# Norms in token halves, an entry block for the rounded operand, and entry parameters behind the first weights

## The reference, cut to what matters

```python
for i in range(2):                                    # first_block
    f = swiglu_ffn(rmsnorm(x, ffn1_norm_pre[i]), ffn1_w_in[i], ffn1_w_out[i])   # ffn1
    x = x + 0.5 * rmsnorm(f, ffn1_norm_post[i])       # post1
    h = rmsnorm(x, mix_norm_pre[i])                   # mix
    ...                                               # p = h @ mix_w_in[i]; delta net, conformer convolution
    x = x + rmsnorm(y, mix_norm_post[i])              # post
    f = swiglu_ffn(rmsnorm(x, ffn2_norm_pre[i]), ffn2_w_in[i], ffn2_w_out[i])   # pre2, ffn2
    x = x + 0.5 * rmsnorm(f, ffn2_norm_post[i])       # post2
h = rms_norm(x, norm1_g)                              # second_block, one layer
...                                                   # proj = h @ w_in; mLSTM and LRU branches
x = x + merged @ w_out
x = x + peer(rms_norm(x, norm2_g), ...)               # 8 heads, 16 experts each, gathered by index
return rms_norm(x, final_norm_g)
```

## Time and profile before

| | us |
|---|---|
| median of 3 runs | 2656.24 |
| the profiled execution | 2657.05 |
| its span, first to last instruction | 2655.8 |
| TensorE matmul busy | 2269.2 (85%) |
| VectorE busy | 1759.4 (66%) |
| ScalarE busy | 970.9 (37%) |
| POOL busy | 807.2 (30%) |

### The profile page before, as it was taken

The page is one execution under the profiler, slowest core; times in us unless marked ns, Lnnn a source line. Parts: engine busy times, 40 slices in busy tenths (PEclk is TensorE's granted clock), DMA queues, the critical chain, the costliest instruction groups (busy, mean ns, idle before and its releaser), DMA issues.

```text
span 2655.8 us, 34386 instructions
## 1 busy us (share of the span) xinstructions
PE 2269.2 (85%) x13786; PEld 1932.1 (73%) x13786; DVE 1759.4 (66%) x3266; ACT 970.9 (37%) x1550; POOL 807.2 (30%) x671
## 2 busy tenths in 40 slices
PE   6999999999999999999999999999898544444445
PEld 6998998998998998998998998888766211111111
DVE  5555894665556556894665555243429998989986
ACT  4345554454335435553454432342213111111111
POOL 1005772000000005771000000000007777777774
PEclk9999999999999999999999999999999677777767
DMA  6567994025554567993024554443249999999997
GB/s 212 183 179 129 188 167 131 33 74 177 183 183 160 188 171 129 187 174 117 33 94 155 184 190 144 141 139 106 74 150 399 419 419 419 419 418 418 419 419 314
DMA packets 316369, 560.29 MB, mean 211 GB/s; under 512 B 16296, under 2 KB 233394, under 8 KB 316210
## 3 DMA queue, kind: packets, MB, share of 16 engines
q1 hardware_dynamic: 242482, 289.63, 39.7%
q0 software_dynamic: 73728, 268.47, 24.9%
HBM read 557.00 MB, written 1.05 MB: 210 GB/s over the span
## 4 chain that ended last, share of the span: by engine, by line
PE 65%; DVE 13%; POOL 8%; DMA 7%; issue 3%; ACT 3%; SPq 0%; DVEq 0%; ACTq 0%; POOLq 0%
PE banks_to L853 11%; PE bank L451 7%; PE bank L452 7%; PE bank L453 7%; PE bank L360 6%; POOL proj L2539 5%; PE banks_and L360 4%; DMA proj<-in_peer_v,gdn_conv 4%; DMA weights<-in_peer_v,gdn_conv 3%; POOL weights L2539 3%; DVE banks_to L1054 3%; PE banks_and L451 3%; PE banks_and L452 3%; PE banks_and L453 3%; PE banks_to L1246 2%
## 5 line engine op out<-in xcount | busy, mean ns | idle before, releaser
L407 POOL TENSOR_TENSOR weights_low<-weights,weights_high 128x1024 fp32r<-128x1024 f32 x128 | 306.1, 2423 | 683.3 <-ACT weights_high L370 682.8
L453 PE MATMUL bank<-operand_hi,weights_low 128*128 128x256 f32 x1792 | 508.5, 284 | 0.0
L451 PE MATMUL bank<-operand_hi,weights_high 128*128 128x256 f32 x1776 | 505.2, 284 | 3.6 <-DVE operand_lo L797 3.3
L452 PE MATMUL bank<-operand_lo,weights_high 128*128 128x256 f32 x1776 | 503.6, 284 | 0.0
L370 ACT CAST weights_high<-weights 128x1024 fp32r<-128x1024 f32 x392 | 386.6, 1046 | 7.0 <-DMA weights<-in_ffn_w_in 6.7
L443 DVE TENSOR_TENSOR weights_low<-weights,weights_high 128x1024 fp32r<-128x1024 f32 x264 | 308.2, 1221 | 91.3 <-ACT weights_high L370 91.3
L451 PEld LDWEIGHTS bank<-operand_hi,weights_high 128*128 128x128 f32 x1776 | 339.1, 191 | 7.0 <-issue 4.7
L453 PEld LDWEIGHTS bank<-operand_hi,weights_low 128*128 128x128 f32 x1792 | 342.9, 191 | 0.0
L452 PEld LDWEIGHTS bank<-operand_lo,weights_high 128*128 128x128 f32 x1776 | 337.5, 190 | 1.3
L453 PE MATMUL banks_and<-operand_hi,weights_low 128*128 128x256 f32 x768 | 217.6, 283 | 0.0
L451 PE MATMUL banks_and<-operand_hi,weights_high 128*128 128x256 f32 x752 | 213.7, 284 | 3.6 <-DVE operand_lo L797 3.3
(11 more groups left out here) (524 smaller groups left out, 4402.6 us busy)
## 6 DMA issues: line engine op xcount, KB each, us to landing
weights<-in_ffn_w_in SPq DMA_DIRECT2D x88, 1024.0 KB, 5.1
weights<-in_mix_w_in SPq DMA_DIRECT2D x64, 1024.0 KB, 12.5
weights<-in_ffn_w_out SPq DMA_DIRECT2D x44, 1024.0 KB, 5.0
weights<-in_w_in SPq DMA_DIRECT2D x24, 1024.0 KB, 5.3
weights<-in_cnv_w_o SPq DMA_DIRECT2D x8, 1024.0 KB, 6.5
weights<-in_gdn_w_o SPq DMA_DIRECT2D x8, 1024.0 KB, 5.2
weights<-in_mix_w_out SPq DMA_DIRECT2D x8, 1024.0 KB, 5.0
weights<-in_peer_w_q SPq DMA_DIRECT2D x8, 1024.0 KB, 5.7
```

Source lines behind the costliest of these rows:

```text
L407: S.rest.by(X.gpsimd.tensor_tensor(halves(m.low[b % SLOTS])[q], halves(m.raw[b % SLOTS])[q], halves(mix_high(m, l, i))[q].bitcast(F32), AL ...
L451: t.matmul(out, w_hi, x_hi, start=start, stop=False, skip_group_check=skip)
L452: t.matmul(out, w_hi, x_lo, start=False, stop=False, skip_group_check=skip)
L453: return t.matmul(out, w_lo, x_hi, start=False, stop=stop, skip_group_check=skip)
```

## The change

Six edits, which touch every boundary.

1. The post-norm interleaves the token halves: VectorE gains half 1 between the two adds of half 0.
2. The norm of the new residual is made for each token half apart (`vector_token_norm`, `scalar_token_norm`): a mean, a root, a reciprocal and a diagonal for each h. In the FFNs it moves ahead of the rounding and the rest of block 2, at the start ahead of those of block 1.
3. The scaled turn goes by pairs of tiles, (0, 1) of both h and then (2, 3) of both h, and all filler products stand before it (20; 12 at norm2). The plain turn keeps its order, with 10 filler products before and 5 between (8 and 8 before).
4. `operand_hi` signals each tile. Block 0 of an FFN or mixer (`tensor_entry_block`) first runs the 32 passes that read the rounded operand, k by k, both column halves, and then the 16 that read `operand_lo`. One clearing flag stands for the whole bank.
5. At the start SP asks for the parameters between weight blocks 0 and 1. TensorE turns the residual first, then 12 filler products, then the parameters, in other banks. VectorE's masks move behind the rest of block 1.
6. POOL computes the rest of a mixer's block 1 only when the post-norm's last add is done.

```diff
+def tensor_entry_block(X, m, S, b, high, low, n):
+    bank, x = b % BANKS, m.split_x
+    X.bank_free(bank)
+    out = lambda q: m.bank[bank][:, q * NT:(q + 1) * NT]
+    for q in range(2):
+        X.pe.wait_ge(*low.at(b, q))
+    for k in range(KT):
+        X.pe.wait_ge(*S.x_high.at(n, k))
+        for q in range(2):
+            hi, lo = halves(high)[q], halves(m.low[b % SLOTS])[q]
+            X.tensor.matmul(out(q), hi[:, k, :], x.hi[:, k, :], start=k == 0 and q == 0, stop=False, skip_group_check=True)
+            X.tensor.matmul(out(q), lo[:, k, :], x.hi[:, k, :], start=False, stop=False, skip_group_check=True)
+    for k in range(KT):
+        if k % 2 == 0:
+            X.pe.wait_ge(*S.x_low.at(n, k // 2))
+        for q in range(2):
+            ins = X.tensor.matmul(out(q), halves(high)[q][:, k, :], x.lo[:, k, :], start=False, stop=k == KT - 1, skip_group_check=True)
+    S.used.by(ins, b)
...
+    vector_gain_branch(X, m, S, n, ready, c, 0)
+    vector_add_branch(X, m, S, n, 0, 0)
+    vector_gain_branch(X, m, S, n, ready, c, 1)
+    vector_add_branch(X, m, S, n, 0, 1)
+    vector_add_branch(X, m, S, n, 1, 0)
+    vector_add_branch(X, m, S, n, 1, 1)
...
+def scalar_token_norm(X, m, S, n, ready, scratch):
+    scalar_token_squares(X, m, S, n, 0, ready, scratch)
+    scalar_token_squares(X, m, S, n, 1, ready, scratch)
+    scalar_token_root(X, m, S, n, 0)
+    scalar_token_root(X, m, S, n, 1)
+
+def vector_token_norm(X, m, S, n):
     for h in range(2):
+        vector_token_mean(X, m, S, n, h)
+    for h in range(2):
+        vector_diagonal(X, m, S, n, h)
...
     tensor_keep_going(X, m, before, first % BANKS)
-    tensor_turn(X, m, S, n, 0, first, ready, scaled)
-    tensor_keep_going(X, m, between, first % BANKS)
-    tensor_turn(X, m, S, n, 1, first, ready, scaled)
+    if scaled:
+        for pairs in ((0, 1), (2, 3)):
+            for h in range(2):
+                tensor_turn(X, m, S, n, first, ready, scaled, h, pairs)
+    else:
+        tensor_turn(X, m, S, n, first, ready, scaled, 0, range(4))
+        tensor_keep_going(X, m, before // 2, first % BANKS)
+        tensor_turn(X, m, S, n, first, ready, scaled, 1, range(4))
...
-    tensor_params(X, m, S, 0)
     for l in range(LAYERS):
-        tensor_to_split(X, m, S, ("pre1", l), ("ffn1", l), x_ready_at(S, l), False, 8, 8 if l else 0)
-        tensor_ffn(X, m, S, ("ffn1", l), split_at(S, ("pre1", l)))
+        tensor_to_split(X, m, S, ("pre1", l), ("ffn1", l), x_ready_at(S, l), False, 10 if l else 0)
+        if not l:
+            tensor_keep_going(X, m, 12, 1)
+            tensor_params(X, m, S, 0)
+        tensor_ffn(X, m, S, ("ffn1", l))
...
-        for i in range(AHEAD):
-            pool_mix_rest(X, m, S, l, i)
-        for i in range(AHEAD, MIX_BLOCKS):
+        pool_mix_rest(X, m, S, l, 0)
+        X.pool.wait_ge(*S.added_dve.at(("post1", l), 1, 1))
+        for i in range(1, MIX_BLOCKS):
             pool_mix_rest(X, m, S, l, i)
```

More of the change, by code:

```diff
@@ L475, in tensor_mix_blocks @@
         b = first + i
-        tensor_split_block(X, m, S, b, mix_high(m, l, b - RING.first["glu", l]), S.rest, m.split_x, ready if i == 0 else ())
+        high = mix_high(m, l, b - RING.first["glu", l])
+        if entry and i == 0:
+            tensor_entry_block(X, m, S, b, high, S.rest, entry)
+        else:
+            tensor_split_block(X, m, S, b, high, S.rest, m.split_x)
         X.free[b % BANKS] = [taken(i)]
@@ new lines, in vector_token_mean, with scalar_token_root @@
+def vector_token_mean(X, m, S, n, h):
+    other = m.sums[:, 4 + 2 * h:5 + 2 * h]
+    X.dve.wait_ge(*S.squares_act.at(n, h, 0))
+    S.mean.by(X.vector.tensor_scalar(other, other, mean_of(1.0), RMS_EPS, ALU.mult, ALU.add), n, h)
+def scalar_token_root(X, m, S, n, h):
+    X.act.wait_ge(*S.mean.at(n, h))
+    X.act.wait_ge(*S.squares_act.at(n, h, 1))
+    S.std.by(X.scalar.activation(m.factors[:, 2 + h:3 + h], m.sums[:, 5 + 2 * h:6 + 2 * h], ACT.Sqrt, bias=m.sums[:, 4 + 2 * h:5 + 2 * h],
+                                 scale=mean_of(1.0)), n, h)
@@ L748, in turn_banks, with tensor_turn @@
     return [3, 4, 5, (first + 2) % BANKS]
-def tensor_turn(X, m, S, n, h, first, ready, scaled):
+def tensor_turn(X, m, S, n, first, ready, scaled, h, pairs):
+    banks = turn_banks(first)
     if scaled:
         X.pe.wait_ge(*S.diagonal.at(n, h))
-    for i, b in enumerate(turn_banks(first)):
+    for i in pairs:
+        b = banks[i]
         if h == 0:
@@ L877, in gated_of, with tensor_ffn @@
     return m.split_gated[1 if j == FF - 1 else 0]
-def tensor_ffn(X, m, S, stage, ready):
+def tensor_ffn(X, m, S, stage):
     w, first = X.pe, RING.first[stage]
@@ L2774, in x_ready_at, with tensor_to_split @@
     return added_at(S, ("post2", l - 1)) if l else lambda h, d: S.x_in.at(0)
-def tensor_to_split(X, m, S, n, stage, ready, scaled, before, between):
-    tensor_boundary(X, m, S, n, RING.first[stage], ready, scaled, before, between)
+def tensor_to_split(X, m, S, n, stage, ready, scaled, before):
+    tensor_boundary(X, m, S, n, RING.first[stage], ready, scaled, before)
     split_taken(X, S, n, RING.first[stage])
```

150 lines of the change are left out of this document (75 added, 75 removed).

## The result

The changed kernel takes 2624.65 us (median of 4 runs, 2623.92 to 2625.36) against 2656.93 (2656.16 to 2658.26) beside it: ratio 0.9878, interval [0.9861, 0.9895]. The profiled execution took 2623.92 with a span of 2622.6, so 33.2 us of span went. Medians are those of runs in the ordinary state: one execution of a variant (`e1_pool_now`) took 3886.11 us at a granted clock of 0.55 and is left out of its median.

A forecast was written before the change was run, and what follows sets the result against it. TensorE, busy 85% of the span, was taken as the bound, its longer waits lying at stage boundaries. Gains 4.8 + 4.8 + 4.8 + 3.1 + 4.0 + 5.1 + 1.0 = 27.6 us off 2656.24 gave 2628.6; range 2618 to 2642.

The forecast's parts named there:

- Start: Kernel start to first output block: parameters land earlier, masks delay VectorE; output block at 40.4 instead of 46.08, 4.8 us gained.
- The charge of 0.9 for clock: At the start, half of one half-clock stretch, charged because TensorE waits twice for about 3 us before the first output block.
- FFN boundaries: Three boundaries into FFN stages: waits behind the plain turn go, and two half-clock stretches with them; 4.8, 4.8, 3.1 us.
- the 0.4 charged for the second diagonal: At FFN boundaries, the factor row was to end 0.4 us later than its usual length because of the second diagonal.
- block 1 is 3.1 earlier: At FFN boundaries, the earlier factor row was to bring block 1 forward by 3.1 us, before 1.7 for clock at two.
- Mixer boundaries: Two boundaries into mixers: adds run free of POOL, each diagonal waits one POOL piece, 1.3 charged for clock; 2.0 us each.
- rival A: No lock at the mixer diagonals, which slip between POOL's pieces: 2 x 4.2 us less, 2620.2 us; chance 0.15.
- norm1: Turn at norm1, POOL idle: earlier diagonal, no filler inside the turn, clock stays full; 5.1 us gained, 1.6 at half clock.
- norm2: Turn at norm2: the 8 filler records inside the turn go, 1.0 us gained.
- Rival C: Behind the boundaries another chain eats the shift; start and five boundaries return 21.5 us, giving 2650; chance 0.04.
- rival D: Slower: at the start the masks meet POOL, 23 mask ops each waiting a piece, 53 us more, near 2680; chance 0.02.
- Rival B: At the boundaries the clock falls to half as often as before; 12.0 us of gain missing, 2640.6; chance 0.24.

The follow-up runs named there:

- e1_pool_now: Against the changed kernel, POOL's copies of the first mixer block no longer wait for the post-norm's last add; 2623.91 us (2622.62 to 2625.10).

## Why the prediction was right, and where its steps were off

Forecast 2628.6, measured 2624.65: inside the range, 27.6 us of gain forecast and 32.3 found. The total came nearer than its steps: two FFN boundaries gave 0.9 and 1.2 less than forecast, the start 2.5 and each mixer 2.0 more, and part of that cancels by luck. Step by step:

- **Start, 4.8 forecast, 7.33 in the profile.** The chain was as forecast: the masks stand in it, and TensorE waits for VectorE behind them. Two sizes were off. The parameters' turn came some 0.7 earlier than the fillers' price of 0.19 let me have it (0.12 from the earlier trace rows was the right row), so operand_hi began 1.1 earlier, the masks ended 1.6 earlier (28.54 for 30.1) and the output block came 1.6 earlier (38.75 for 40.4). The charge of 0.9 for clock belongs behind the first output block, where one of the two profiles paid 1.57.
- **FFN boundaries, 4.8, 3.1 and 4.8 forecast, 3.56, 3.60 and 3.89 found.** The factor row starts 3.6 earlier, forecast 3.4, and lasts its usual 0.71: the 0.4 charged for the second diagonal was not paid. The half-clock stretches of both pre2 boundaries went, as forecast. The 3.1 + 1.7 came as 3.56 and 3.89 since the step that failed is "block 1 is 3.1 earlier", taken on to the output block: in these two stages the parameter copies end last, 1.41 and 0.91 late. With them moved the second FFN gains 5.2. The weight I gave to the causes was off as well: I began with block 0's earlier start, but that is worth nothing in the second FFN, 0.18 in the fourth and 1.39 in the third, while without the root's new place all three lose their whole gain. The two are not a sum: block 0's order counts only where nothing behind it waits for another engine.
- **Mixer boundaries, 2.0 forecast, 4.06 and 4.01.** The lock at the diagonals came (rival A is out): 1.33 and 2.19 us, where I had let the second one end 0.6 later. That is 0.75 of the difference; the other 1.3 is the clock stretch that I charged and that did not fall into either profile. It does fall there in five of the variants that keep the fillers. The diagonal takes 0.29 alone and 1.33 or 2.19 beside POOL, and held apart it is 0.29 again. The Trainium skill (SBUF — State Buffer, Who interferes with whom) states the rule: a tensor_scalar in a two-port mode and a GpSimd instruction exclude each other for the whole instruction, whichever is issued first. The trace agrees.
- **norm1, 5.1 forecast, 5.58**: no half clock, a first product 3.67 behind the turn's start instead of 8.34.
- **norm2, 1.0 forecast, 1.24.** Rival C (the shift is eaten on the way) is refuted by the equal lengths between boundaries; rival D's collision did not occur, the masks ran in 5.6 us. Rival B, that half clock stays, is wrong for this kernel's two profiles but not for its neighbours: seven of the eleven variants have stretches in boundary lengths, at 1.5 to 2.8 us each where the fillers stand and 0.55 to 1.57 without them.

**Which boundaries lose the clock.** The same instructions have a stretch at a mixer boundary in one kernel and none in the next. The kept traces sort them. Within each profile the moments at which the granted clock changes lie on an even grid, to 0.005 us, and that grid lies differently against the program from profile to profile. Seven profiles have the mixer boundary as in the changed kernel up to the end of the turn (its own two, the two of the masks, the copies, block 0, the root), 14 boundaries. In the six with a stretch the turn starts 0.95 to 2.28 us behind a point of the grid; in the eight without one it starts under 0.46 or over 2.5 us behind one. With POOL held until the diagonal, in three kernels, none of the six boundaries has a stretch, although three start their turn 1.8 to 2.4 us behind a point: there TensorE's wait ahead of the turn is 0.74 us and the second is gone, in place of 1.79 and 1.14. With the post-norm's old order, whose wait ahead of the turn is 2.23, both boundaries have one, at 2.70 and 0.52. Without fillers the first mixer's turn starts 0.01 us behind a point, where the boundaries with fillers had no stretch, and it has one; so the fillers hold the clock there, as at norm1. For the second mixer (1.88) the run cannot tell. The sorting was read off afterwards, and no run set the offset on purpose. The Trainium skill (TensorE: Matmul & The Clock Gate, Part 1: The HAM clock gate) says that the window by which the gate is set is free-running and does not reset when a kernel starts; the two profiles of the changed kernel, with the start's stretch at 16.52 and at 39.01, agree with it.

What stays open: the start's 7.3 us are not split between SP's new order and TensorE's, the turn by pairs of tiles has no run of its own, and of norm1's 5.58 only the interleaving's 0.49 has a run that takes it back.

## What to carry to other kernels

Before crediting an earlier start of a block, follow it to the next thing that waits for another engine: an edit hidden by such a wait is worth nothing until the wait goes, and then its full price. Work held back from one collision lands on the next instruction; put the release behind the last instruction that can collide. Where medians move by whole half-clock stretches, compare lengths between marks of the traces, with the share of each that ran at half clock.

## What the runs showed that I had not expected

A half-clock stretch of 3.4 us costs 1.6 in a dense part, while two of 6.8 us cost 0.55 and 1.28 where TensorE was waiting for much of them (busy 3.17 and 4.75 us). Boundary lengths between marks repeat within 0.03 us in different kernels on different chips as long as the clock is equal. The collision with POOL also takes the add, which reads two tiles besides a scalar column: 2.04 us instead of 0.75.
